# Two transformer blocks on one core: modulation parts summed in one bank, attention values and branch lifts made turned, first input product by block, first query in halves

## The chip, the core and the metric

The kernel runs on one core of a Trainium2 chip. The core has five engines that run their own instruction streams and meet at semaphores: PE (matrix products, PSUM as its output), DVE (vector work), ACT (scalar functions), POOL (here: a little arithmetic and the gathers) and SP (it issues the other DMAs). The metric is the device time of one execution in microseconds. All arithmetic is float32; the profile shows each PE product as two records.

PSUM is one tensor `ps` of 8 banks of 128 x 512 values. The main buffer in the core's memory is `big`; the program's tiles are ranges of it, so the profile writes `big` for most of them.

## What is computed

The reference, cut to its parts that the change touches:

```python
def first_block(x, ...):                      # x: 1 x 256 x 1024
    h = rmsnorm(x, norm_mix)
    aq, ak, av, hq, hf_f, hf_b, hi, hg, gate_pre = split(h @ w_in)
    ...                                       # norms and rotary positions of q, k
    y_att = gqa_attention(q, k, v) @ w_up_att     # 8 heads, 2 groups, width 64
    y_hg = hgrn2_bidirectional(...) @ w_up_hg
    gts = sigmoid(gate_pre)                   # two gates of width 1024
    merged = gts[0] * y_att + gts[1] * y_hg
    x = x + merged @ w_out
    x = x + peer_ffn(rmsnorm(x, norm_ffn), ...)
    ...
def peer_ffn(h, w_q, sub_keys, u, v):         # per token: 8 heads x 16 experts of 16384
    q = h @ w_q
    s = einsum(q, sub_keys)                   # 8 heads x 2 halves x 128 scores
    idx, g = ...                              # top 16 of sums of two top 16
    a = <u[idx], h>;  w = gelu(a) * g;  return sum of w * v[idx]
def second_block(x, c, ...):
    mod = silu(c) @ w_ada + b_ada             # 6 parts of 1024
    sh_m, sc_m, gt_m, sh_f, sc_f, gt_f = split(mod)
    h = modulate(rms_norm(x, g_mix), sh_m, sc_m)
    ...                                       # mixer, then a gated feed-forward
```

## The kernel before

The 256 tokens are two blocks of 128 rows (`NB`), the width 1024 is eight chunks of 128 (`KD`). One layer of each block is computed. Nothing is scheduled by a program: every engine's stream is written by hand, and PE's order is repeated in `product_list`. That list numbers every result that PE leaves in a bank; `product_done` counts them, `bank_list` deals them to banks in turn (eight ahead of the query, then four, since two pairs of banks hold the sums of the experts), and `begin` waits until the bank's last user has emptied it (`bank_emptied`). `wait_product` and `wait_moved` are the waits for a result and for its removal.

**Weights.** `tile_list` is the order of the weight tiles, each up to 1024 x 512 values (2.1 MB). They go through a ring of three slots (`wring`, `W_SLOTS`). SP issues them in that order (L442) and waits before each until the tile that held the slot has had its last product. `w_up_hg` (L435) and the `subkeys` (L440) have places of their own and stand in the same queue. x, the lane constants and the identity are issued ahead of the first tile `in_hf`.

**The first stage** up to the query runs on PE in this order: the normed x turned (`n1T`), products of h with the tiles of `w_in`, by columns of the weight (`by_cols`, L509: the weight is stationary and 256 tokens move, the result is turned) or by rows (`by_rows`, L497: 512 columns of the weight move, tokens on the partitions). Then attention: scores `a_S` (L558), ACT's exponentials, transposes of the probabilities (`probs_turned`, L548), values (`attended`, L570: eight heads x two blocks of keys, 64 columns each), DVE divides by the sums (`attention_in`), and PE turns the result (`attended_turned`, L579). Then the eight levels of the gated scan (`level`, L589), with the products of the branch gates `in_g0` to `in_g3` between them, `g_O` (L662), a norm on DVE and ACT, and its transposes `g_OT` (L673).

Spread among these are eight parts of `mod` that are needed as columns: `ada_part(i)` (L523) multiplies silu(c), repeated 32 times in `c_rep`, with a tile, four chunks at a time on four 32-column strips of the array, which leaves partial sums on the partitions; ACT moves them out, and `ada_col(i)` (L531) adds the four strips and turns them with four products of one column. Four more parts are needed as rows, in the second block (`ada8` to `ada11`).

`lifted(b, h)` (L686) makes the two lifts of block b, half h, by rows; DVE combines them with the gates into `merged`, PE turns it (`turn_merged`, L486), ACT moves it to `hT`, and `out0`, `out1` follow by rows.

**The query.** DVE adds `out0` and `out1` to x, ACT and DVE norm it, PE turns it (`turn_query`), and `query("peer_q0", 0)` (L716) and `score(0, 0)` (L727) make the scores of the first two heads. ACT moves both. DVE's `route_first(0)` finds the experts of head 0 of all 128 rows (from L1668 on) and writes 16 indices a row. From these POOL starts gathers (L1364), each of one pair of expert rows for 128 tokens, 1.05 MB, into a ring of ten slots. Gathers 0 to 9 wait for indices alone (the tenth also for `out1` of block 1). Gather 10 waits until PE has used the first pair. Per batch of four pairs DVE makes the dot products (L1763), ACT the diagonals (L1185), PE the products (`experts`, L747), and a bit of the next heads' search and query stands between the batches. PE's order ahead of the first `experts` is `peer_q0`, `keys`, `out1` of block 1, `peer_q1`, `keys`, `peer_q2`, `residual` (L754). The slot of `peer_q2` is the one that `out1` leaves.

## Time and profile before

| | |
|---|---|
| median of 3 runs | 1412.82 us (1412.06 to 1413.28) |
| profiled execution | 1411.05 us |
| its span, first to last instruction | 1409.0 us |
| PE busy | 1273.0 us, 90% |
| DVE, POOL, ACT busy | 52%, 23%, 17% |
| mean granted clock of PE | 0.964 |

The profiled execution is 1.8 us under the median, and 2.05 us of it lie outside the span. A granted clock of 1.00 is the 2.4 GHz level of PE, 0.50 the 1.2 GHz level. In the tables a row gives the start and the length of a group of like instructions, and in brackets how long its engine had been idle and what ended that.

### The profile page before, as it was taken

How to read it: one execution, taken by the hardware profiler on the slowest of the kernel's cores; microseconds unless marked ns; L12 is line 12 of the kernel's file. 1: busy time of each engine (PE TensorE's matmuls, PEld its weight loads, DVE VectorE, ACT ScalarE, POOL GpSimd, SP SyncE). 2: the span in 40 equal slices, each digit the busy share in tenths (PEclk: the TensorE clock that was granted, in tenths of full speed). 3: DMA queues.
4: the chain of work that ended last, by engine and by line, in shares of the span. 5: the costliest groups of instructions: out<-in, count | busy, mean ns of one | idle time of the engine just before them, and what ended most of it. 6: DMA issues, size and time to landing. Idle time of an engine off the chain costs nothing.

```text
span 1409.0 us, 12608 instructions
## 1 busy us (share of the span) xinstructions
PE 1273.0 (90%) x4558; PEld 730.9 (52%) x4558; DVE 726.7 (52%) x1752; ACT 238.8 (17%) x611; POOL 324.6 (23%) x273
## 2 busy tenths in 40 slices
PE   7999999988988878788799887878999899999998
PEld 6757554574554444333333333333465468988743
DVE  3664623178777777787786865653255242100001
ACT  2132221121111111112221112112112421000000
POOL 0100000024544544354444454540000000000000
PEclk9999999999999999899999998999999989999999
DMA  8534576369999999999999999995344723552530
GB/s 289 176 123 180 179 277 245 120 269 421 390 419 421 421 416 420 416 421 401 417 422 421 411 415 421 420 422 216 120 166 166 263 78 120 179 180 95 204 145 34
DMA packets 98380, 398.72 MB, mean 283 GB/s; under 512 B 6353, under 2 KB 9809, under 8 KB 65425
## 3 DMA queue, kind: packets, MB, share of 16 engines
q0 software_dynamic: 37376, 270.29, 46.4%
q1 hardware_dynamic: 60944, 127.65, 25.4%
q8 instruction: 37, 0.61, 0.2%
q14 instruction: 23, 0.18, 0.0%
HBM read 396.86 MB, written 1.05 MB: 282 GB/s over the span
## 4 chain that ended last, share of the span: by engine, by line
PE 60%; DMA 22%; DVE 12%; issue 2%; ACT 2%; POOL 1%; DVEq 0%; SPq 0%; ACTq 0%
DMA big<-in_peer_uv,idx_t 21%; PE ps L497 16%; PE ps L509 14%; PE ps L747 11%; DVE big L1763 6%; PE ps L998 5%; PE ps L716 2%; PE ps L686 2%; PE ps L962 2%; PE ps L523 1%; PE ps L589 1%; POOL big L1364 1%; PE ps L486 1%; DMA wring<-in_w_ada 1%; ACT rows L1185 1%
## 5 line engine op out<-in xcount | busy, mean ns | idle before, releaser
L747 PE MATMUL ps<-big,rows 128*128 128x512 f32 x1024 | 489.0, 634 | 105.4 <-ACT rows L1185 105.4
L1364 POOL DMA_INDIRECT big<-in_peer_uv,idx_t x256 | 312.0, 1219 | 388.9 <-PE ps L747 323.5
L747 PEld LDWEIGHTS ps<-big,rows 128*128 128x128 f32 x1024 | 202.7, 203 | 374.0 <-issue 374.0
L1763 DVE CUSTOM_DVE_ANT_0 big<-big 128x1024 f32<-128x1024 f32 x256 | 307.8, 1225 | 145.5 <-DMA big<-in_peer_uv,idx_t 142.5
L497 PE MATMUL ps<-wring,big 128*128 128x512 f32 (+1 forms) x560 | 240.5, 586 | 2.6 <-DMA wring<-in_w_in 1.1
L509 PE MATMUL ps<-big,wring 128*128 128x256 f32 x896 | 195.7, 381 | 1.0 <-DVE big L1418 1.0
L509 PEld LDWEIGHTS ps<-big,wring 128*128 128x128 f32 x896 | 171.2, 191 | 25.3 <-issue 1.9
L497 PEld LDWEIGHTS ps<-wring,big 128*128 128x128 f32 x560 | 105.6, 191 | 125.8 <-issue 121.0
L1179 ACT ACTIVATE small<-small 128x4 f32<-128x4 f32 x64 | 13.2, 206 | 514.7 <-DVE small L1768 514.7
L1185 ACT ACTIVATE rows<-const,small 128x128 f32<-128x128 f32 x256 | 81.8, 390 | 19.2 <-DVE small L1772 18.0
L998 PE MATMUL ps<-wring,big 128*128 128x512 f32 x176 | 75.7, 592 | 0.0
L716 PEld LDWEIGHTS ps<-big,wring 128*128 128x128 f32 x512 | 63.6, 199 | 14.6 <-issue 13.6
L716 PE MATMUL ps<-big,wring 128*128 128x128 f32 x512 | 64.8, 283 | 4.6 <-issue 3.7
L1043 ACT ACTIVATE big<-ps 128x512 f32<-128x512 f32 x73 | 40.9, 592 | 153.7 <-PE ps L486 61.7
L998 PEld LDWEIGHTS ps<-wring,big 128*128 128x128 f32 x176 | 33.4, 190 | 41.7 <-issue 41.6
L1956 DVE SCALAR_TENSOR_TENSOR big<-ps,big 128x512 f32<-128x512 f32 x8 | 5.5, 692 | 93.1 <-PE ps L998 70.6
L1987 DVE TENSOR_TENSOR big<-big,ps 128x512 f32<-128x512 f32 x11 | 7.6, 688 | 82.1 <-PE ps L509 74.8
L1375 POOL TENSOR_TENSOR big<-big,rows 128x1024 f32<-128x1024 f32 x2 | 4.7, 2342 | 149.8 <-ACT big L1043 142.9
L1343 POOL DMA_DIRECT2D rows<-in_norm_ffn x1 | 0.7, 686 | 149.1 <-DVE big L1625 149.1
L1984 DVE SCALAR_TENSOR_TENSOR big<-big,ps 128x512 f32<-128x512 f32 x11 | 7.6, 688 | 46.9 <-ACT big L1327 46.9
L1327 ACT ACTIVATE big<-ps 128x512 f32<-128x512 f32 x11 | 6.6, 597 | 136.4 <-DVE big L1987 63.3
L962 PEld LDWEIGHTS ps<-big,wring 128*128 128x128 f32 x256 | 28.8, 192 | 0.5 <-issue 0.5
(241 smaller groups left out, 921.9 us busy)
## 6 DMA issues: line engine op xcount, KB each, us to landing
wring<-in_w_in SPq DMA_DIRECT2D x17, 2048.0 KB, 8.3
wring<-in_w_ada SPq DMA_DIRECT2D x12, 2048.0 KB, 8.5
wring<-in_w_gate SPq DMA_DIRECT2D x5, 2048.0 KB, 7.7
wring<-in_w_up SPq DMA_DIRECT2D x5, 2048.0 KB, 7.7
wring<-in_w_down SPq DMA_DIRECT2D x5, 2048.0 KB, 7.6
wring<-in_w_out SPq DMA_DIRECT2D x4, 2048.0 KB, 15.1
wring<-in_peer_wq SPq DMA_DIRECT2D x4, 2048.0 KB, 8.0
big<-in_peer_uv,idx_t POOLq DMA_INDIRECT x256
```

What stands on the lines that cost most here:

```text
L486: last = nc.tensor.transpose(o[:, c * P:(c + 1) * P], src[:, b, (4 * h + c) * P:(4 * h + c + 1) * P], ident)
L497: last = nc.tensor.matmul(o[:, 0:w], lhs[:, c, b * P:(b + 1) * P], wt[:, c, c0:c0 + w], start=(c == 0), stop=(c == k - 1))
L509: last = nc.tensor.matmul(o[:, c2 * S:(c2 + 1) * S], wt[:, c, n0:n0 + P], src[:, c, :], start=(c == 0), stop=(c == KD - 1))
L686: last = nc.tensor.matmul(o, lhs[:, c, b * P:(b + 1) * P], wt[:, c, h * 512:(h + 1) * 512], start=(c == 0), stop=(c == 3))
L716: last = nc.tensor.matmul(o[:, n * P:(n + 1) * P], wt[:, c, n * P:(n + 1) * P], h2T[b][:, c, :], start=(c == 0), stop=(c == KD - 1))
L747: last = nc.tensor.matmul(banks[h], diag[:, k % DIAGS, :], v_part[:, ring_at(k), h * 512:(h + 1) * 512], start=False, stop=(k % SLOTS == S ...
L962: last = nc.tensor.matmul(o[:, c2 * S + b * P:c2 * S + (b + 1) * P], wt[:, c, n0:n0 + P], hT2[:, c, b * P:(b + 1) * P], start=(c == 0), st ...
L998: last = nc.tensor.matmul(o, gT[:, f, b * P:(b + 1) * P], wt[:, c, h * 512:(h + 1) * 512], start=(f == 0), stop=(f == FC - 1))
L1043: nc.scalar.activation(dst, bank(name, n) if src is None else src, ACT.Copy).then_inc(emptied(*name), 1)
L1185: nc.scalar.activation(diag[:, k % DIAGS, :], ident, ACT.Copy, scale=w_now[:, at_w:at_w + 1])\
L1364: pool.indirect_dma_start(pair_ring[:, ring_at(k), :], None, a["peer_uv"], bass.IndirectOffsetOnAxis(idx_t[:, k:k + 1], 0))\
L1763: nc.vector.tensor_tensor_reduce(u_part[:, ring_at(k), :], u_part[:, ring_at(k), :], h_t[:, b, :], 1.0, 0.0, ALU.mult, ALU.add, a_dot[:, i ...
```

## The change

- **Modulation parts.** `c_wide` has 40 columns a chunk, zero but for column 8. Taking 32 of them from column 8 - i on puts silu(c) on partition i of each strip. So parts 0 to 7 are added into one bank (bank 7, which nothing else uses up to the query; the others are dealt to seven banks). One move, one group of four products against `part_sums` and one more move make all eight. The slot of a part 0 to 6 is now freed by a count of its own, `ada_used`.
- **Attention values turned.** DVE multiplies the probabilities with the reciprocals ahead of their transposes (`normalised`), and `attended` makes the values turned: per block of keys and group one product of 512 columns, on the upper or lower 64 partitions of the result. ACT moves it to `yT`. `attention_in` and `attended_turned` go.
- **Lifts turned.** `in_g0` to `in_g3` and both lifts are made by columns, DVE combines them straight in `hT`, and the transposes of `merged` go. The second half of `in_g3` moves behind `g_O`, `ada6` behind `g_OT`, `ada7` among the lifts. `out0` of block 0 starts when three of four parts of `merged` are there, and `out0` of block 1 is split around the query's transposes.
- **First input product by block.** `in_hf` is made for block 0 before block 1 is turned, and x's second block is issued behind the tile `in_hf`.
- **First query in halves.** `peer_q0` and its scores for block 0 are made, moved and searched one head at a time.

The core of the diff:

```diff
@@ product_list
+    p += [("g_O", 0), ("g_O", 1), ("in_g3", 1), ("g_OT", 0), ("g_OT", 1)]
+    p += [("up_hg", 0), ("up_hg", 1), ("up_att", 0), ("ada7",), ("up_att", 1)]
+    p += [("up_hg", 2), ("up_att", 2), ("up_hg", 3), ("up_att", 3)]
...
@@ SP
-            sp.dma_start(x[:, 1, :], a["x"][P:S, :]).then_inc(x_landed[1], 16)
             sp.dma_start(ident, a["const"][:, C_IDENT:C_IDENT + P]).then_inc(ident_landed, 16)
...
-                    if before.startswith("down"):
+                    if before.startswith("ada") and int(before[3:]) < ADA_COLS - 1:
+                        sp.wait_ge(ada_used, int(before[3:]) + 1)
+                    elif before.startswith("down"):
...
+                if n == 0:
+                    sp.dma_start(x[:, 1, :], a["x"][P:S, :]).then_inc(x_landed[1], 16)
@@ PE
             def ada_part(i):
                 wt = tile(f"ada{i}", KD, 512)
-                o = begin(f"ada{i}")
+                cols_ = i < ADA_COLS
+                o = ps[:, BANK[("ada7",)], :] if i < ADA_COLS - 1 else begin(f"ada{i}")
+                lo = ADA_COLS - i if cols_ else ADA_COLS
...
-                last.then_inc(product_done, 1)
-
-            def ada_col(i):
-
-                wait_moved(pe, f"ada{i}")
-                o = begin("ada_col", i)
+                last.then_inc(ada_used if i < ADA_COLS - 1 else product_done, 1)
+
+            def ada_col():
+
+                wait_moved(pe, "ada7")
+                o = begin("ada_col")
...
                 o = begin("a_Y", b)
-                for h in range(AH):
-                    for s_b in range(NB):
-                        g = h % 2
-                        last = nc.tensor.matmul(o[:, h * HD:(h + 1) * HD], a_PT[:, s_b, h, :],
-                                                qkv[:, s_b, 640 + g * HD:640 + (g + 1) * HD],
+                for s_b in range(NB):
+                    for g in range(AKV):
+                        last = nc.tensor.matmul(o[g * HD:(g + 1) * HD, :],
+                                                qkv[:, s_b, 640 + g * HD:640 + (g + 1) * HD], a_PT[:, s_b, g:AH:AKV, :],
                                                 start=(s_b == 0), stop=(s_b == NB - 1))
                 last.then_inc(product_done, 1)
-
-            def attended_turned(b):
-                pe.wait_ge(a_out, b + 1)
...
+            by_block("in_hf", 0, hT)
+            pe.wait_ge(h_ready, 2)
+            turn("n1T", h_t, [1])
+            wait_turned("n1T", [1])
+            by_block("in_hf", 1, hT)
...
+            reserved("out0", 1)
+            merged_out(0, 1, range(0, 5))
             turn_query(0)
+            begin("out0", 1)
+            merged_out(0, 1, range(5, 8)).then_inc(product_done, 1)
             wait_turned("n2T", [0])
-            query("peer_q0", 0)
...
+            o = begin("peer_q0", 0, 0)
+            first_query(0, o)
+            first_query(1, o).then_inc(product_done, 1)
+            first_query(2, reserved("peer_q0", 0, 1))
             pe.wait_ge(keys_landed, 16)
-            score(0, 0)
+            first_score(0)
+            first_query(3, begin("peer_q0", 0, 1)).then_inc(product_done, 1)
+            first_score(1)
             by_rows("out1", hT, blocks=[1])
@@ DVE
+            def normalised(b):
                 for n in range(4):
                     wait_moved(dve, "a_S", b, n // 2, n % 2)
                 s8 = sum1[:, 8 * b:8 * b + 8]
                 link(nc.vector.reciprocal(s8, s8))
+                tt(a_P[:, b], a_P[:, b], s8.unsqueeze(2).to_broadcast([P, AH, S]), ALU.mult).then_inc(a_normed, 1)
```

How PE's order moves, in two places. First from the first half of `in_g3` and the last level to the first lifts. Before (L523 is `ada_part`, L531 `ada_col`, L497 the second half of `in_g3`, L662 `g_O`, L673 `g_OT`, L686 the lifts):

```order
L497 MATMUL ps<-wring,big 128x512 x8
L523 MATMUL ps<-wring,c_rep 32x512 x8
L531 MATMUL ps<-const,big 128x1 x4
L662 MATMUL ps<-big 128x128 x16
L523 MATMUL ps<-wring,c_rep 32x512 x8
L531 MATMUL ps<-const,big 128x1 x4
L523 MATMUL ps<-wring,c_rep 32x512 x8
L531 MATMUL ps<-const,big 128x1 x4
L673 MATMUL ps<-const,big 128x128 x8
L531 MATMUL ps<-const,big 128x1 x4
L686 MATMUL ps<-wring,big 128x512 x4
L686 MATMUL ps<-big 128x512 x4
```

And in the changed kernel (L526 `ada_part`, L667 `g_O`, L510 the second half of `in_g3`, L675 `g_OT`, L690 the lifts, those with `wring` being `up_att`):

```order
L526 MATMUL ps<-wring,c_wide 32x512 x16
L667 MATMUL ps<-big 128x128 x16
L510 MATMUL ps<-big,wring 128x256 x16
L675 MATMUL ps<-const,big 128x128 x8
L526 MATMUL ps<-wring,c_wide 32x512 x8
L690 MATMUL ps<-big 128x256 x16
L690 MATMUL ps<-big,wring 128x256 x8
L526 MATMUL ps<-wring,c_wide 32x512 x8
L690 MATMUL ps<-big,wring 128x256 x8
```

The second half of `in_g3` now stands behind `g_O`, and with it the moment at which its slot is free for `ada7`, behind which `up_att` is queued on SP.

Second, PE from `out0` of block 0 to `peer_q1`. Before (L497 rows of `out0`, `out1`, L486 transposes, L716 query, L727 scores):

```order
L497 MATMUL ps<-wring,big 128x512 x8
L486 MATMUL ps<-const,big 128x128 x8
L497 MATMUL ps<-wring,big 128x512 x16
L486 MATMUL ps<-const,big 128x128 x8
L716 MATMUL ps<-big,wring 128x128 x32
L727 MATMUL ps<-big 128x128 x4
L497 MATMUL ps<-wring,big 128x512 x8
L716 MATMUL ps<-big,wring 128x128 x32
```

And in the changed kernel (L710 products of `out0`, L536 `ada_col`, L498 `out1`, L758 and L766 the first query and its scores, L733 `peer_q1`):

```order
L710 MATMUL ps<-wring,big 128x512 x5
L487 MATMUL ps<-const,big 128x128 x8
L710 MATMUL ps<-wring,big 128x512 x3
L758 MATMUL ps<-big,wring 128x128 x24
L766 MATMUL ps<-big 128x128 x2
L758 MATMUL ps<-big,wring 128x128 x8
L766 MATMUL ps<-big 128x128 x2
L498 MATMUL ps<-wring,big 128x512 x8
L733 MATMUL ps<-big,wring 128x128 x32
```

The scores of the first head now stand ahead of the last quarter of the query; `out1` of block 1 and all behind it keep their places.

## Rows read from the trace of the kernel before

**Rows 1.** The page, DMA rate in 40 equal slices of the span.

```profile
GB/s 289 176 123 180 179 277 245 120 269 421 390 419 421 421 416 420 416 421 401 417 422 421 411 415 421 420 422 216 120 166 166 263 78 120 179 180 95 204 145 34
```

**Rows 2.** The page, chain that ended last, share of the span by engine.

```profile
PE 60%; DMA 22%; DVE 12%; issue 2%; ACT 2%; POOL 1%; DVEq 0%; SPq 0%; ACTq 0%
```

**Rows 3.** Groups by form, PE, 0 to 340 us: busy, mean ns, idle before.

```profile
L716 PE MATMUL ps<-big,wring 128*128 128x128 f32 x208 | 27.8, 295 | 4.6 <-issue 3.7 <-ACT big L1043 0.8
...
L523 PE MATMUL ps<-wring,c_rep 128*32 128x512 f32 x128 | 15.4, 598 | 0.0
...
L531 PE MATMUL ps<-const,big 128*128 128x1 f32 x64 | 8.5, 253 | 0.0
...
L570 PE MATMUL ps<-big 128*128 128x64 f32 x64 | 7.4, 275 | 0.0
...
L673 PE MATMUL ps<-const,big 128*128 128x128 f32 x8 | 1.3, 286 | 1.4 <-DVE big L1633 1.4
...
L579 PE MATMUL ps<-const,big 128*128 128x128 f32 x8 | 1.0, 272 | 0.0
```

**Rows 4.** Timeline of PE at the first lifts: start, length, group.

```profile
220.42 0.66 PE L673 MATMUL ps<-const,big 128*128 128x128 f32 x4 [1.39 <-DVE big L1633]
...
222.17 6.61 PE L686 MATMUL ps<-wring,big 128*128 128x512 f32 x8
228.61 3.60 PE L686 MATMUL ps<-big 128*128 128x512 f32 x8
```

**Rows 5.** Windows: length, busy PE, PEld, DVE, ACT, POOL, PEclk, DMA, GB/s.

```profile
222.00:223.00 1.00, 1.00 (x3) 0.65 (x4) 0.00 (x0) 0.17 (x1) 0.23 (x1) 0.50 0.92 365
```

**Rows 6.** Start of the program: timeline of PE, then one window.

```profile
13.30 29.42 PE L509 MATMUL ps<-big,wring 128*128 128x256 f32 x128 [1.02 <-DVE big L1418]
...
0.00:10.00 10.00, 1.94 (x8) 1.57 (x8) 2.95 (x7) 6.17 (x12) 0.18 (x4) 1.00 0.81 285
```

**Rows 7.** Two tiles issued together: SP's first issue, window at the end.

```profile
186.03 0.37 SPq L435 DMA_DIRECT2D big<-in_w_up_hg  x1
...
198.00:199.00 1.00, 1.00 (x12) 0.13 (x4) 0.18 (x1) 0.00 (x0) 0.00 (x0) 1.00 0.40 135
```

**Rows 8.** Timeline of PE: peer_q0, first records of peer_q2, residual.

```profile
276.82 7.38 PE L716 MATMUL ps<-big,wring 128*128 128x128 f32 x64 [0.79 <-ACT big L1043]
...
302.16 3.85 PE L716 MATMUL ps<-big,wring 128*128 128x128 f32 x33
...
316.99 1.88 PE L754 MATMUL ps<-x_t,const 128*128 128x512 f32 x4
```

**Rows 9.** Issues: POOL's gathers 0 and 10; SP's tile peer_q2.

```profile
296.85 1.04 POOL L1364 DMA_INDIRECT big<-in_peer_uv,idx_t  x1 [42.06 <-DVE idx_t L1721]
...
320.86 0.95 POOL L1364 DMA_INDIRECT big<-in_peer_uv,idx_t  x1 [11.60 <-PE ps L747]
...
L442 SPq DMA_DIRECT2D wring<-in_peer_wq x1: 368/368/368, 293.0 to 293.0; - x1
```

**Rows 10.** Timeline of DVE ahead of the first search.

```profile
268.33 0.69 DVE L1655 SCALAR_TENSOR_TENSOR x_t<-ps,x_t 128x512 f32<-128x512 f32 x1 [6.98 <-PE ps L497]
270.93 1.28 DVE L1411 SCALAR_TENSOR_TENSOR big<-x_t,rstd,rows 128x1024 f32<-128x1024 f32 x1 [1.91 <-ACT rstd L1039]
...
286.73 0.29 DVE L1668 MAX8 big<-big 128x8 f32<-128x128 f32 x1 [10.84 <-ACT big L1043]
```

**Rows 11.** DMA queues (packets, MB, share): 294 to 297, 299 to 300, 375 to 377.

```profile
q1 hardware_dynamic: 405, 0.83, 85.8%
...
q0 software_dynamic: 3, 0.02, 6.3%
...
q0 software_dynamic: 92, 0.66, 78.5%
q1 hardware_dynamic: 92, 0.19, 24.1%
```

**Rows 12.** Timeline of PE in the expert stage, after a longer idle stretch.

```profile
434.90 8.80 PE L747 MATMUL ps<-big,rows 128*128 128x512 f32 x16 [2.15 <-ACT rows L1185]
```

More of the change, by code:

```diff
@@ L58 @@
 C_GROUP = C_ONE + 1
[L59 removed]
+C_PART = C_GROUP + P
+C_END = C_PART + ADA_COLS
 L_LB = 0
@@ L651, in _ @@
                     ada_part(i + 1)
-                if n % 2 == 0 and i:
-                    ada_col(i + 1)
-            by_rows("in_g3", hT, blocks=[1])
             ada_part(5)
-            ada_col(4)
             pe.wait_ge(g_filled, 1)
@@ L664, in _ @@
                 last.then_inc(product_done, 1)
-            ada_part(6)
-            ada_col(5)
-            ada_part(7)
-            ada_col(6)
+            by_cols("in_g3", halves=[1])
             for b in range(NB):
@@ L674, in _, with lifted @@
                 last.then_inc(product_done, 1)
[L675 removed]
+            ada_part(6)
             for b in range(NB):
[L678 removed]
                 wait_moved(pe, "g_OT", b)
[L680 removed]
             pe.wait_ge(up_hg_landed, 16)
[L682 to L684 removed]
+            def lifted(name, h):
+                lhs, wt = (yT, tile("up_att", 4, D)) if name == "up_att" else (oT, up_hg)
+                o = begin(name, h)
+                for c2 in range(2):
+                    n0 = (2 * h + c2) * P
@@ L694, in _ @@
-            lifted(0, 0)
-            lifted(0, 1)
-            lifted(1, 0)
-            turn_merged(0)
-            lifted(1, 1)
-            wait_turned("mT", [0])
-            by_rows("out0", hT, blocks=[0])
-            turn_merged(1)
+                last.then_inc(product_done, 1)
+            lifted("up_hg", 0)
+            lifted("up_hg", 1)
+            for b in range(NB):
+                wait_moved(pe, "a_Y", b)
+            lifted("up_att", 0)
+            pe.wait_ge(const_landed, 32)
@@ new lines, in _, with merged_out @@
+            ada_part(7)
+            lifted("up_att", 1)
+            for h in (2, 3):
+                lifted("up_hg", h)
+                lifted("up_att", h)
+            def merged_out(i, b, chunks):
+                wt = tile(f"out{i}", KD, 512)
+                o = ps[:, BANK[(f"out{i}", b)], :]
+                for c in chunks:
+                    last = nc.tensor.matmul(o, hT[:, c, b * P:(b + 1) * P], wt[:, c, :], start=(c == 0),
+                                            stop=(c == KD - 1))
+                return last
@@ L702, in _ @@
+            reserved("out0", 0)
+            pe.wait_ge(merged_ready, 3)
+            merged_out(0, 0, range(0, 6))
+            pe.wait_ge(merged_ready, 4)
+            begin("out0", 0)
+            merged_out(0, 0, range(6, 8)).then_inc(product_done, 1)
+            ada_col()
             by_rows("out1", hT, blocks=[0])
-            wait_turned("mT", [1])
-            by_rows("out0", hT, blocks=[1])
             def turn_query(b):
@@ L1192, in _ @@
             query_turned(0)
-            query_out(0, 0)
-            scores_out(0, 0)
+            for h in range(2):
+                c = slice(2 * h, 2 * h + 2)
+                for name, dst in ((("peer_q0", 0, h), pqT), (("keys", 0, 0, h), sc[(0, 0)])):
+                    move(dst[:, c, :], *name, src=bank(name, 2 * P).rearrange("p (c t) -> p c t", c=2))
             best(0)
```

245 lines of the change are left out of this document (111 added, 134 removed).

## Prediction, made before the run

> **What bounds the kernel now.** I read the page first: its 40 slices and the chain that ended last. In the slices the rate of the DMA engines is the thing to see [rows 1]. It goes up and down until the tenth slice, stands at 390 to 422 GB/s from there to slice 27, and falls again. The chain that ended last is mostly PE [rows 2], and between 332 and 971 us it alternates between gathers, dot products and PE. So there are three stages. Up to the first gather at 296.85 us [rows 9] PE is busy nearly without a break. From there to about 966 us, 256 gathers of 1.05 MB pass at the rate of the DMA engines. After that PE is the bound again, and the change moves nothing there that I can price above zero: `c_wide` is as wide in a product as `c_rep` was, and the products of `gate0` and `up0` are the same code under another name. Work taken from PE ahead of the first gathers moves everything behind it, if the gathers are fed as before. That "if" is the second half of this prediction.
>
> I sum against the profiled execution (1411.05 us) and add 1.8 us at the end, since the median is 1412.82. Q is the start of the first query product, 276.82 us now [rows 8].
>
> **PE ahead of Q: what goes.** The rows by form give the busy time of each kind [rows 3]. A group overlaps the next by some 0.1 us, and I subtract that.
> - Attention values: 64 records of 64 columns take 7.4 us, the same 275 ns as a record of 128 columns, so narrow products are paid in full. Now it is 4 products a block of 512 columns on 64 columns of the array, and the two groups can run beside each other. No row shows column tiles of 64. Bounds: `ada_part` on tiles of 32 takes 1.9 us for 16 records (15.4 us for 128), which is four at once; with no overlap, 8 records of 0.43 us are 3.4. I take 1.9 us a block, a saving of 3.3 in all; the other end is 0.1.
> - `ada_col`: 8.5 us for eight groups, 7.6 without overlap. One group of four stays: -6.6.
> - Transposes: those of the attention values (L579, 1.0 us of records, 0.9 net) and of `merged` (twice as many, 1.8): -2.7.
> - The idle 1.4 us ahead of the second `g_OT` transposes [rows 3, 4]. They come 7.7 us after `g_O` ends, by a chain of DVE and ACT that stays. Now 6.9 us of `in_g3` and 0.45 of the first transposes stand in that gap: -1.0.
> - Behind that idle time the granted clock is 0.50, the 1.2 GHz level, and 8 records of the first lift take 6.61 us where the next 8 take 3.60 [rows 4, 5]. With the gap filled by dense products I take this away: -3.2. The other end is nothing.
> - The 0.8 us in which PE waited for ACT ahead of the query [rows 3] is covered by three products of `out0`: -0.8. DVE adds `out1` of block 0 at 268.33, 0.2 after the product, and ends the scaled row for the query at 272.2 [rows 10], 4.1 after the product; five products of `out0` take 4.3, so PE just doesn't wait for it.
>
> Together 17.6 us.
>
> **PE ahead of Q: what comes.**
> - `in_hf` by block. PE begins it now at 13.30, when both blocks are turned [rows 6]. Later it begins when block 0 is turned (about 9.7 us) and the tile has landed. By 10 us the engines have moved 2.85 MB [rows 6]. Without x's second block ahead of it the tile ends at 2.75 MB, so at 9.75 us; I add 1.3 us until the landing is seen, an assumption: 11.0. Half of the tile's products take 7.1, 1.8 more at the low clock, then 2.4 for the second block's transposes and their moves, then 7.1: the end is 29.5 instead of 28.9. +0.6, between -0.7 and +1.5.
> - `ada5` is now used 12.3 us after the last of `in_g2`, and is the second of two tiles issued then. The pair issued at 186.03 ended on the DMA engines at 198.4 [rows 7], 12.4 us later, and lands about 0.5 after: +0.4.
> - `up_att` is the larger one. Its transfer stands in SP's queue behind `ada7`, which needs `in_g3`'s slot, and `in_g3`'s last product has moved behind `g_O`. So both tiles are issued at that product's end, and `up_att` lands 12.7 us later by the same pair. PE needs it after 0.45, 0.4 idle, 0.45, `ada6` 1.85 and two lifts 6.9, that is after 10.1. +2.6. Nothing on PE can pass it. An idle stretch of 2.15 us elsewhere is followed by 16 records in 8.80 us, where two times 3.60 less the overlap make 7.0 [rows 4, 12]: +1.8.
> - Lifts, gate products by columns, DVE's two products with the reciprocals (2.4 us each, in front of transposes that have 4 us to spare) and ACT's extra table loads cost nothing: PE's own work hides them. Uncovered, the two DVE products would be 4.8.
>
> Together 5.4 us. So Q and all up to `out1` of block 1 come **12.2 us earlier**.
>
> The Trainium skill ("TensorE: Matmul & The Clock Gate", Measured speedup vs the span model) has three column tiles at 2.38 times the speed of one, 0.79 of ideal. Two tiles at 0.79 would take 2.2 us instead of 1.9, and the sum would be 0.6 us worse; `ada_part`'s own row is nearer to ideal, and I stay with it.
>
> **The query in halves.** DVE starts its search now 9.9 us after Q (286.73) [rows 10]. With halves it is 3.6 for two products' worth, 1.8 for the third, which hides ACT's move, 0.7 for half of the scores and 0.45 for their move: 6.6. The search takes 9.8 us either way, so the first gather is issued at Q+16.7 instead of Q+20.0.
>
> One might take these 3.3 us as a gain. But the DMA engines are full from 294.75 on, first with `peer_q2`, whose slot is free when `out1` of block 1 is done (issued at 293.0 [rows 9]). The first bytes of a gather appear only at 299.9 [rows 11], and `peer_q2` ends at 300.3: it had a lead of 5.1 us and passed alone. The engines' full stretch starts no earlier relative to Q, so the earlier gathers bring nothing, and they take `peer_q2`'s lead: 2.1 us are left, in which 0.77 of its 2.10 MB pass (0.83 MB by 297.0 now [rows 11]). Beside gathers a tile gets 0.19 MB in 2 us, equal packets but small ones [rows 11]. The other 1.33 MB need 13 to 14.5 us, and it lands at Q+34 to Q+35. PE wants it at Q+25.3 (302.16) [rows 8]. A **stall of about 9 us** on PE.
>
> Behind it: 7.1 for the products, some 2.2 for the low clock after such a gap, 1.7 for the residual, and the first expert products free a ring slot, 2.2 after which gather 10 is issued: Q+47.5. Now that is Q+44.0 (320.86) [rows 9], since today the same products take 14.8 us, from 302.16 to 316.99 [rows 8], with 3.7 us of idle time that nothing shown ends [rows 3]. If these 3.7 come again, it is Q+51.2. The ten gathers and the tile are 12.6 MB and end at Q+48.1; gather 10's bytes come 3.0 after its issue. So the engines stand idle 2.2 to 5.9 us, and the next batch, which has under 1 us to spare, loses some more. **+4.5 us**, which the engines don't make up.
>
> Sum: 1411.05 - 12.2 + 4.5 + 1.8 = 1405.2.
>
> The skill ("DMA: Bandwidth & Descriptors", Queues, rings and completion order) has the engines take turns between queues by the packet. By that rule the tile gets its share in packets, and the rows have 92 against 92; an equal share by bytes would leave a stall of under 2 us and give some 1401.
>
> **Rivals.**
> - No collision: the tile keeps enough of its lead, or PE's stall is hidden by DMA engines that are full anyway. For it: each microsecond of lead is worth 4.5 us of transfer. Then the 4.5 fall away: 1400.7.
> - The removals are worth less: the 64-column tiles don't overlap (3.2 us) and the clock still falls at `g_OT` (3.2), because the same short transposes stand there. 1411.6.
> - The tile loses its whole lead. This is the slower one. Decisive point: the first gather's bytes come no later than the tile's, that is 2.1 us sooner than I put them. All 2.10 MB then pass at 0.09 MB/us, landing at Q+41.8; with the low clock and the 3.7 us again, gather 10 is issued at Q+58.7, 14.7 later than now. 1411.05 - 12.2 + 14.7 + 1.8 = 1415.4. Against it: SP issues the tile at Q+15.9, and a gather's first bytes took 3.0 us [rows 9, 11].
>
> **How the numbers follow.** Forecast 0.62, no collision 0.20, smaller removals 0.12, lead lost 0.06. The range takes the forecast's ends, the block-wise `in_hf` and the collision from 2.2 to 9, and reaches past the first rival and short of the second: 1399.5 to 1411.0. A measurement of this kernel can tell about 0.2%, 2.8 us, from no change. Faster by more: 0.84, from the first two cases less the forecast's slow tail, and a little of the third. Within: 0.11. Slower: 0.05.
>
> **What the profile after would show.** `a_Y` groups of about 1.9 us; no idle time at `g_OT` over 0.5 and a clock of 1.00 there; a PE wait of about 2.6 us for a tile in the middle of the lifts; Q near 264.6; the first gather 16.7 after Q; PE idle about 9 us ahead of `peer_q2`'s products, the tile's bytes running beside gathers at a quarter of the rate; a dip of the DMA engines some 48 us after Q; the stage behind 971 us unchanged at 438 us. I am wrong on the whole if the dip is missing or much longer, or if Q isn't 10 us or more earlier.

## Result, and the profile after

| | before | after |
|---|---|---|
| median, us | 1412.87 (1412.06 to 1413.28) | 1405.45 (1404.28 to 1406.13) |
| ratio, 95% interval | 1 | 0.9945 (0.993 to 0.996) |
| profiled execution, us (span) | 1411.05 (1409.0) | 1405.89 (1403.7) |
| start of the first query product (Q) | 276.82 | 268.19 |
| gather 0 issued | 296.85 = Q+20.0 | 284.73 = Q+16.5 |
| gather 10 issued | 320.86 = Q+44.0 | 313.97 = Q+45.8 |
| last gather issued | 954.72 | 948.46 |

The change makes the kernel 7.4 us faster, which is 0.2 us from the forecast. The profile shows that this closeness is in part luck: two terms of opposite sign were both too large, by some 3 us each. By the prediction's own last sign ("if Q isn't 10 us or more earlier") it was wrong on the whole: Q is 8.6 us earlier. Medians are used below for what an edit is worth, the traces for where it goes.

The page of after has the three stages of before: DMA rate in 40 slices, then the chain that ended last.

```profile
GB/s 286 158 147 180 180 263 261 128 357 393 404 420 421 421 415 420 418 421 411 421 420 421 394 411 421 422 421 172 120 169 164 262 81 122 180 179 100 200 148 32
...
PE 57%; DMA 24%; DVE 12%; issue 2%; ACT 2%; POOL 1%; another core or an unknown queue 1%; SPq 0%; DVEq 0%
```

Against [rows 1], the engines fill earlier (357 where 269 stood in the ninth slice), and the tenth slice is lower (393 for 421). The first is the gain, the second is where a part of it goes.

PE's groups by form, 0 to 340 us: busy, mean ns, idle before. They answer to [rows 3].

```profile
L604 PE MATMUL ps<-big,wring 128*128 128x128 f32 x128 | 17.6, 307 | 3.6 <-DMA wring<-in_w_in 2.7 <-DVE big L1433 1.0
L690 PE MATMUL ps<-big,wring 128*128 128x256 f32 x64 | 16.3, 414 | 2.9 <-DMA wring<-in_w_up_att 2.9
...
L526 PE MATMUL ps<-wring,c_wide 128*32 128x512 f32 x128 | 15.4, 598 | 1.4 <-DMA wring<-in_w_ada 1.4
...
L573 PE MATMUL ps<-big 128*64 128x512 f32 x16 | 3.9, 605 | 0.0
...
L744 PE MATMUL ps<-big 128*128 128x128 f32 x16 | 3.1, 358 | 8.8 <-ACT big L1071 8.8
...
L675 PE MATMUL ps<-const,big 128*128 128x128 f32 x8 | 1.3, 279 | 0.3 <-DVE big L1644 0.3
...
L536 PE MATMUL ps<-const,big 128*128 128x8 f32 x8 | 1.0, 246 | 0.0
```

The attention values (L573) cost 3.9 us where 7.4 stood. `ada_col` (L536) costs 1.0 for 8.5. The transposes of `g_OT` (L675) wait 0.3 for 1.4. In their place come waits for tiles: 2.7 at `in_hf`, 1.4 at an ada part, 2.9 at `up_att`, and 8.8 at a score product.

PE's timeline at these places: `in_q` behind `in_hb` (of before, then of after), `ada5`, the lifts, the first query product, the scores of `peer_q1`.

```profile
42.56 20.80 PE L497 MATMUL ps<-wring,big 128*128 128x512 f32 x64
```

```profile
44.72 20.80 PE L498 MATMUL ps<-wring,big 128*128 128x512 f32 x64
...
195.39 1.92 PE L526 MATMUL ps<-wring,c_wide 128*32 128x512 f32 x16 [1.42 <-DMA wring<-in_w_ada]
...
211.19 7.17 PE L690 MATMUL ps<-big 128*128 128x256 f32 x32
221.29 5.38 PE L690 MATMUL ps<-big,wring 128*128 128x256 f32 x16 [2.93 <-DMA wring<-in_w_up_att]
...
228.45 3.72 PE L690 MATMUL ps<-big,wring 128*128 128x256 f32 x16
...
268.19 5.52 PE L758 MATMUL ps<-big,wring 128*128 128x128 f32 x48
...
299.92 2.07 PE L744 MATMUL ps<-big 128*128 128x128 f32 x8 [8.78 <-ACT big L1071]
```

The start of after is 2.2 us later than that of before at `in_q`, so the removals gave 8.6 + 2.2 = 10.8 us net of the other waits. The issues of gathers 0 and 10 on POOL, ACT's move that PE waited for, windows of the dip behind gather 10 (length, busy time of PE, PEld, DVE, ACT, POOL, granted clock, DMA share, GB/s), and the two queues at 290 to 292 us:

```profile
284.73 1.04 POOL L1379 DMA_INDIRECT big<-in_peer_uv,idx_t  x1 [27.88 <-DVE idx_t L1745]
...
313.97 1.60 POOL L1379 DMA_INDIRECT big<-in_peer_uv,idx_t  x1 [16.83 <-PE ps L789]
...
299.27 0.60 ACT L1071 ACTIVATE big<-ps 128x512 f32<-128x512 f32 x1 [11.82 <-remote]
...
314.00:317.00 3.00, 3.00 (x9) 1.33 (x8) 3.00 (x7) 0.00 (x0) 2.69 (x2) 1.00 0.95 325
317.00:320.00 3.00, 3.00 (x17) 2.04 (x16) 1.77 (x8) 0.23 (x1) 2.39 (x3) 1.00 0.92 371
...
q0 software_dynamic: 82, 0.67, 81.2%
q1 hardware_dynamic: 80, 0.16, 21.5%
```

The tile of `peer_q2` (queue q1) passes beside the gathers (q0) with as many packets and a fifth of the bytes, as forecast. The dip is there too: 325 and 371 GB/s where [rows 1] has 421. But it is small: 0.44 MB under 421 GB/s from 314 to 320 us, worth about 1.0 us. What the forecast hadn't is ACT's idle time of 11.8 us, which ends by nothing that the profile knows. It means that PE in this execution stood 8.8 us ahead of the scores, for ACT, and never for the tile itself. Is it that, or the tile, which costs the time? And is the collision worth 4.5 us?

### The profile page after: what moved, and what is told of

Its sections match the earlier page's. It is cut to its first block, busy times and chain, and to the rows that moved or that the text cites. A ratio compares the mean times of both kernels' runs of the same rounds, so it can differ in the third digit from the quotient of the medians.

```text
span 1403.7 us, 12831 instructions
## 1 busy us (share of the span) xinstructions
PE 1257.9 (90%) x4686; PEld 752.9 (54%) x4686; DVE 730.3 (52%) x1753; ACT 234.1 (17%) x597; POOL 321.2 (23%) x273
## 4 chain that ended last, share of the span: by engine, by line
PE 57%; DMA 24%; DVE 12%; issue 2%; ACT 2%; POOL 1%; another core or an unknown queue 1%; SPq 0%; DVEq 0%
DMA big<-in_peer_uv,idx_t 20%; PE ps L510 16%; PE ps L789 11%; PE ps L498 11%; DVE big L1787 6%; PE ps L1026 5%; PE ps L604 3%; DMA wring<-in_w_ada 2%; PE ps L690 2%; DMA wring<-in_w_in 1%; PE ps L733 1%; PE ps L526 1%; PE ps L710 1%; DMA wring<-in_w_up_att 1%; POOL big L1379 1%
## 5 line engine op out<-in xcount | busy, mean ns | idle before, releaser
L1379 POOL DMA_INDIRECT big<-in_peer_uv,idx_t x256 | 308.6, 1205 | 384.3 <-PE ps L789 336.2
L510 PE MATMUL ps<-big,wring 128*128 128x256 f32 x1088 | 237.0, 379 | 0.0
L510 PEld LDWEIGHTS ps<-big,wring 128*128 128x128 f32 x1088 | 205.9, 190 | 29.7 <-issue 2.2
L498 PE MATMUL ps<-wring,big 128*128 128x512 f32 (+1 forms) x400 | 169.3, 580 | 2.8 <-ACT big L1071 1.6
L498 PEld LDWEIGHTS ps<-wring,big 128*128 128x128 f32 x400 | 75.6, 191 | 88.6 <-issue 83.7
L1199 ACT ACTIVATE rows<-const,small 128x128 f32<-128x128 f32 x256 | 81.8, 390 | 19.2 <-DVE small L1796 18.0
L733 PEld LDWEIGHTS ps<-big,wring 128*128 128x128 f32 x448 | 54.5, 196 | 9.1 <-issue 9.1
L1026 PEld LDWEIGHTS ps<-wring,big 128*128 128x128 f32 x176 | 33.4, 190 | 41.7 <-issue 41.6
L1071 ACT ACTIVATE big<-ps 128x512 f32<-128x512 f32 (+1 forms) x64 | 34.9, 577 | 123.0 <-PE ps L498 30.3
L733 PE MATMUL ps<-big,wring 128*128 128x128 f32 x448 | 54.7, 279 | 0.0
L604 PE MATMUL ps<-big,wring 128*128 128x128 f32 x384 | 46.5, 286 | 3.6 <-DMA wring<-in_w_in 2.7
L604 PEld LDWEIGHTS ps<-big,wring 128*128 128x128 f32 x384 | 46.1, 202 | 4.7 <-issue 3.5
```

The source lines that it names most:

```text
L498: last = nc.tensor.matmul(o[:, 0:w], lhs[:, c, b * P:(b + 1) * P], wt[:, c, c0:c0 + w], start=(c == 0), stop=(c == k - 1))
L510: last = nc.tensor.matmul(o[:, c2 * S:(c2 + 1) * S], wt[:, c, n0:n0 + P], src[:, c, :], start=(c == 0), stop=(c == KD - 1))
L604: last = nc.tensor.matmul(o[:, c2 * S + b * P:c2 * S + (b + 1) * P], wt[:, c, n0:n0 + P], src[:, c, b * P:(b + 1) * P], start=(c == 0), st ...
L733: last = nc.tensor.matmul(o[:, n * P:(n + 1) * P], wt[:, c, n * P:(n + 1) * P], h2T[b][:, c, :], start=(c == 0), stop=(c == KD - 1))
L1026: last = nc.tensor.matmul(o, gT[:, f, b * P:(b + 1) * P], wt[:, c, h * 512:(h + 1) * 512], start=(f == 0), stop=(f == FC - 1))
L1071: nc.scalar.activation(dst, bank(name, n) if src is None else src, ACT.Copy).then_inc(emptied(*name), 1)
```

## Experiments

"The changed kernel" is after. Readings of all runs stand in one table. MB is what the DMA engines moved from 280 to 600 us, the sum of windows of 20 us. At some 0.42 MB/us it tells how far the stage of the gathers has come at 600 us. The ratios go by runs of before that were taken beside each set, with medians of 1412.01 us (e1 to e4), 1411.88 (e5 to e8) and 1411.83 (e9 to e12); so medians of different sets compare only to about 1 us.

| run | edit | median, us | ratio to before (95%) | Q | gather 10 | MB to 600 |
|---|---|---|---|---|---|---|
| before | | 1412.87 | | 276.82 | Q+44.0 | 127.8 |
| after | | 1405.45 | 0.9945 (.993-.996) | 268.19 | Q+45.8 | 130.2 |
| e8 | after once more | 1404.31 | 0.9938 (.9923-.9952) | 267.66 | Q+45.3 | 130.9 |
| e1 | query whole | 1403.51 | 0.9941 (.9928-.9955) | 267.26 | Q+42.8 | 131.6 |
| e2 | before, query halved | 1413.30 | 1.0014 (1.0002-1.0026) | 277.35 | Q+45.0 | 128.0 |
| e4 | tile ahead of gathers | 1406.46 | 0.9963 (.995-.9977) | 267.31 | Q+46.4 | 130.0 |
| e3, e10 | `in_hf` whole | 1408.98, 1408.45 | 0.9984 (.9975-.9993), 0.9975 (.9965-.9986) | 268.63, 270.69 | Q+44.7, 45.3 | 130.7, 129.7 |
| e12 | ACT's program shifted | 1402.81 | 0.9932 (.9914-.9949) | 267.10 | Q+44.4 | 131.1 |
| e5 | `up_att` ahead | 1399.61 | 0.9911 (.9898-.9925) | 263.11 | Q+46.4 | 132.3 |
| e6 | `ada5` first | 1401.66 | 0.9923 (.9909-.9936) | 264.89 | Q+45.7 | 131.7 |
| e9 | halves, both orders | 1398.26 | 0.9901 (.9885-.9918) | 262.90 | Q+43.9 | 133.3 |
| e7, e11 | whole, both orders | 1397.82, 1398.72 | 0.9895 (.988-.991), 0.9905 (.9889-.9922) | 261.68, 261.33 | Q+42.6, 43.1 | 133.9, 134.0 |

**The query whole again (e1).** `peer_q0` of block 0 goes back to one bank, one product and one score.

```diff
-            o = begin("peer_q0", 0, 0)
-            first_query(0, o)
...
-            first_score(1)
+            query("peer_q0", 0)
+            pe.wait_ge(keys_landed, 16)
+            score(0, 0)
```

> The changed kernel with its first query and scores whole again, as in the kernel before (PE, ACT and DVE); all else as changed. Q stays at 268.2 us. Collision theory: with the whole query the tile of peer_q2 is issued at about Q+16.2 and the first gather at Q+20.0, so the tile keeps its lead of 5 us, lands by about Q+24.5, PE's stall of 8.8 us ahead of keys(0,1) and peer_q2 goes to under 1 us, gather 10 is issued at about Q+44, and the time falls by the 4.5 us that the stage lost: about 1401.0 us. Rival A, the halves bring what they were meant to (the first gather 3.3 us earlier) and the stage's loss comes from elsewhere: 3.3 us slower than the changed kernel, about 1408.7. Rival B, the loss belongs to ACT's idle time of 11.8 us that has its own cause (it was 3.05 us in the kernel before): the stall comes again in this kernel and the time stays within 1 us of 1405.5.

The tile's wait is gone, as the collision has it. In PE's timeline the products of `peer_q2` follow the scores at once, but the experts' first products then wait for ACT. Gather 10 and the same windows as above:

```profile
292.13 7.31 PE L733 MATMUL ps<-big,wring 128*128 128x128 f32 x64
299.28 1.88 PE L776 MATMUL ps<-x_t,const 128*128 128x512 f32 x4
306.29 8.64 PE L769 MATMUL ps<-big,rows 128*128 128x512 f32 x16 [5.14 <-ACT rows L1179]
...
310.06 0.94 POOL L1357 DMA_INDIRECT big<-in_peer_uv,idx_t  x1 [10.44 <-PE ps L769]
...
314.00:317.00 3.00, 2.70 (x19) 1.98 (x17) 0.24 (x3) 1.14 (x3) 1.45 (x2) 1.00 1.02 423
```

No dip: 423 GB/s where after has 325. At 600 us it is 1.4 MB ahead of after, 3.3 us, and 0.9 of them are its earlier Q. That leaves 2.4 us for the halves in these two executions, and 1.3 against e8 (0.7 MB, less 0.4). The medians give less: 0.9941 against 0.9945 and 0.9938 is nothing that can be told from zero. That the halves take the tile's lead is shown, the price of 4.5 us is not.

**Before, with only the query halved (e2).** The same lines, the other way.

```diff
-            query("peer_q0", 0)
-            pe.wait_ge(keys_landed, 16)
-            score(0, 0)
+            o = begin("peer_q0", 0, 0)
+            first_query(0, o)
...
+            first_score(1)
```

> The kernel before with only the first query and its scores in halves, as in the changed kernel; nothing else of the change. Q stays at 276.8 us. Collision theory: first gather at about Q+16.7, tile of peer_q2 beside gathers, PE waits some 9 us for it, gather 10 comes 2 to 6 us later against Q than the 44.0 of before, and the time rises by about 4.5 us: 1417.3 us. Rival A (the earlier first gather is a gain): 3.3 us less, 1409.5. Rival B (the loss has nothing to do with the halves): within 1 us of 1412.8.

PE waits for the tile itself here, 6.6 us:

```profile
308.80 9.86 PE L716 MATMUL ps<-big,wring 128*128 128x128 f32 x64 [6.58 <-DMA wring<-in_peer_wq]
```

At 340 us this kernel is 0.7 MB behind before (19.2 to 19.9). At 380 us it is 0.2 ahead (35.9 to 35.7). What before has in hand it loses itself, a little later: one window of before, then the same of this kernel.

```profile
360.00:380.00 20.00, 19.37 (x67) 10.65 (x68) 15.84 (x49) 5.44 (x16) 10.42 (x8) 0.91 0.93 374
```

```profile
360.00:380.00 20.00, 17.87 (x69) 10.25 (x70) 15.85 (x53) 5.65 (x17) 9.92 (x9) 1.00 1.01 411
```

Both sums run from 280 us. The ring of ten gathers, which PE, DVE and ACT must turn over, loses something against 421 GB/s between 320 and 380 us in every kernel here: 1.0 MB in before, but only 0.2 to 0.4 in the others with the query whole (e7, e11, e1), and 0.7 to 1.2 in those with halves, e4 aside (0.2). So in this pair the collision's loss takes the place of another, and "which the engines don't make up" was wrong; in the pair of e1 and after there is little other loss that could cover it. Gather 10 comes at Q+45.0, only 1.0 us later than in before. By the ratio the time is 2.0 us over before (0.3 to 3.7), by the two medians of this set 1.3: less than half of the forecast's 4.5.

**The tile ahead of the gathers (e4).**

```diff
+                if k == 0:
+                    n_q2 = TILE_NO["peer_q2"]
+                    pool.wait_ge(tile_landed[n_q2 % W_SLOTS], 16 * (n_q2 // W_SLOTS + 1))
```

> The changed kernel with one wait more: GpSimd issues gather 0 only when the tile of peer_q2 has landed. Collision theory: the tile passes alone in about 5.3 us and lands at about Q+21.6 (289.8 us), PE's stall ahead of peer_q2 goes, the first gather is issued 5 us later and its first bytes come 3.0 us after that, in which the DMA engines stand idle; gather 10 isn't late any more. Net of the two about 1.5 us less than the changed kernel, 1404.0, and 3 us more than with the whole query. On ACT: if its idle time of 11.8 us ahead of the move of peer_q1's product comes from the load on the DMA engines by gathers and tile together, it is under 4 us here; if it has another cause, it is there again with 10 us or more, PE waits for it again, and the time is 3 to 5 us above the changed kernel's, since the gathers start later.

The window in which the DMA engines stand nearly idle, then PE's timeline:

```profile
290.00:295.00 5.00, 4.31 (x39) 4.12 (x38) 4.62 (x19) 2.58 (x4) 2.63 (x3) 1.00 0.35 97
```

```profile
291.95 7.31 PE L733 MATMUL ps<-big,wring 128*128 128x128 f32 x64
299.09 1.88 PE L796 MATMUL ps<-x_t,const 128*128 128x512 f32 x4
309.72 8.96 PE L789 MATMUL ps<-big,rows 128*128 128x512 f32 x16 [8.74 <-ACT rows L1199]
```

The wait for the tile is gone and stands one product later: the first experts have no gathered rows yet, and gather 10 comes at Q+46.4, later than in after. It is 1 to 3.5 us slower than the changed kernel (1405.45 and, in another set, 1404.31 us) and not 1.5 faster. Protecting the tile in this way costs no less than the collision does. ACT's idle time ahead of the move is 3.75 us here, not 11.8.

**ACT's 11.8 us (e8, e12).** e8 is the changed kernel itself; e12 has 32 waits more in ACT's program, on a semaphore long at its value, where ACT stands idle.

```diff
             log_and_exp()
+            for _ in range(32):
+                act.wait_ge(lane_landed, 16)
```

> The changed kernel itself once more, beside the others on one chip. Expected 1405.4 us. Every theory that has ACT's 11.8 us of idle time ahead of peer_q1's move as a property of this kernel expects it again at 287 to 299 us. The other theory: it belongs to the one execution, since the kernels with the query whole and with the tile first have nothing like it; then ACT moves peer_q1's product at about 291.2 us here, PE waits 6 to 7 us for the tile itself, and the time is the same within 1 us because the tile was late in both.

> The changed kernel with 32 more wait instructions in ACT's program, on a semaphore that is long at its value, where ACT stands idle (behind the move of ada_col): only the place of what follows in ACT's program changes. Theory A, ACT's idle time of 11.8 us ahead of the move of peer_q1's product is the loading of its next instructions beside the gathers: it is gone from there or stands at another instruction, ACT moves the product at about 291.5 us, and PE waits 6 to 7 us for peer_q2's tile itself. Theory B, it belongs to this move (a semaphore or a port): 11.8 us again at the same instruction. Either way the tile holds PE until about 299 to 300 us, and the time is within 1 us of the changed kernel's 1404.3.

ACT's timeline of e8, of e12 and of e9 at this move, then PE's in e12:

```profile
298.69 0.60 ACT L1071 ACTIVATE big<-ps 128x512 f32<-128x512 f32 x1 [11.77 <-remote]
```

```profile
290.09 0.60 ACT L1071 ACTIVATE big<-ps 128x512 f32<-128x512 f32 x1 [3.74 <-PE ps L733]
```

```profile
285.89 0.60 ACT L1074 ACTIVATE big<-ps 128x512 f32<-128x512 f32 x1 [3.74 <-PE ps L736]
```

```profile
298.23 9.54 PE L733 MATMUL ps<-big,wring 128*128 128x128 f32 x64 [6.33 <-DMA wring<-in_peer_wq]
```

The idle time isn't of one execution alone: 11.82 in after, 11.77 in e8, 11.82 in e5, 11.76 in e6. With 32 waits in front of the place it is gone. But that doesn't show that the place in ACT's program decides. The edits of e3, e10, e4 and e9 touch PE, SP or POOL alone and leave ACT's program as it is in the changed kernel, and there too ACT moves the product 3.7 us after its last work, as soon as PE has made it. e9 differs from e5, which has the idle time, only in the place of one issue on SP some 90 us earlier, and the DMA engines are as full; a packet of the queue q14, of kind instruction, passes between 288 and 289 us in both. So neither theory is shown and neither is excluded: the cause of the 11.8 us stays open. In e12 PE waits 6.3 us for the tile. `peer_q2` starts at 298.23 in e12 and at 301.20 in e8, and Q differs by 0.6. So the idle time had up to 2.4 us of its own in the trace, and gather 10 comes 1.0 us nearer to Q. At 600 us e12 is 0.2 MB ahead, which its earlier Q explains; the medians, 1402.81 and 1404.31, are nearer than the intervals can part. What the idle time costs in the end can't be told from zero.

**`in_hf` whole (e3, e10).** x's second block is issued ahead of the first tile, both blocks are turned, and the products go over both.

```diff
-            by_block("in_hf", 0, hT)
...
-            turn("n1T", h_t, [1])
-            wait_turned("n1T", [1])
-            by_block("in_hf", 1, hT)
+            by_cols("in_hf")
```

> The changed kernel with in_hf as before: x's second block issued ahead of the first weight tile, both blocks turned, then the products by columns over both blocks. Theory from the trace (in_hb began at 30.9 us in the changed kernel and at 28.7 before): in_hb begins 2.2 us earlier, everything behind it up to the first query too, and the time is 2.2 us less than the changed kernel's, about 1403.2. By the forecast's own term (0.6) it would be 1404.9; the rival is that the 2.2 us are taken up by a wait later (for a tile of the input products or for DVE), so the time stays at 1405.5.

> The changed kernel with in_hf whole, once more, for a second profile: the first profile was of the fastest of its executions (span 1403.9, the others up to 1410.4). Theory: in_hf by block and in_hf whole give the same Q, since the waits for ada5 and up_att take up what PE is early (in the first profile 1.9 and 4.2 us against 1.4 and 2.9): Q at 268 to 269 again, and a median at the level of the changed kernel, 1404 to 1406. Rival: the median of 1409.0 is a property of this kernel; then the profile shows where 4 us go, in a longer wait for a tile ahead of Q or in a longer stage of the gathers.

The 2.2 us didn't come, and the kernel is some 4 us slower than the changed one (0.9984 and 0.9975 of before, against 0.9945 and 0.9938), though the changed kernel didn't run in either of these two sets. It begins `in_q` at 43.4 and 42.7 us, up to 2.0 earlier than after. PE's timeline of e3 and of e10 at `ada5` and `up_att`:

```profile
194.58 1.92 PE L525 MATMUL ps<-wring,c_wide 128*32 128x512 f32 x16 [1.90 <-DMA wring<-in_w_ada]
...
221.72 5.38 PE L686 MATMUL ps<-big,wring 128*128 128x256 f32 x16 [4.19 <-DMA wring<-in_w_up_att]
```

```profile
194.15 3.58 PE L525 MATMUL ps<-wring,c_wide 128*32 128x512 f32 x16 [2.18 <-DMA wring<-in_w_ada]
...
222.76 6.41 PE L686 MATMUL ps<-big,wring 128*128 128x256 f32 x16 [3.98 <-DMA wring<-in_w_up_att]
```

Being early buys a longer wait for `ada5`. In e10 that wait is 2.2 us, and behind it the granted clock is 0.50, the 1.2 GHz level; in e3 it is 1.9 us and the clock stays. The same microsecond, of e10 and of e3:

```profile
195.00:196.00 1.00, 1.00 (x12) 0.34 (x8) 0.00 (x0) 0.00 (x0) 0.00 (x0) 0.50 1.05 408
```

```profile
195.00:196.00 1.00, 1.00 (x16) 0.26 (x8) 0.00 (x0) 0.00 (x0) 0.00 (x0) 1.00 0.97 356
```

The part takes 3.58 us for 1.92, the last product of `in_g3` and with it the issue of `up_att` come later, and Q is as late as 270.7. The executions of this kernel spread more than those of after (spans 1403.7 to 1410.4 us). The profiled one of e3 was the shortest of its eleven, that of e10 the longest of its ten; that others lost their clock in the same way fits, but wasn't seen. There is a second piece. PE starts on `up_att` 14.1 and 13.9 us after its issue in e3 and e10, and 12.9 to 13.0 after it in after, e1, e4, e8 and e12. In the first two, and in none of the other five, a packet of another queue passes in that stretch, at 212 to 214 us of e3:

```profile
q8 instruction: 1, 0.02, 3.3%
```

3.3% of 16 engines in 2 us is 1.06 us of one engine, the size of the delay. That is two executions of one kernel against five of others, not an experiment.

**SP's order (e5, e6), and all together (e7, e11, e9).** In e5 `up_att`, whose slot `ada5` leaves at 197 us, is issued ahead of `ada7`, which has to wait for `in_g3`. The loop then goes over `issued`:

```diff
+            issued = list(enumerate(TILES))
+            i = TILE_NO["ada7"]
+            issued[i:i + 2] = issued[i + 1], issued[i]
```

In e6 `up_hg` is issued behind `ada5`:

```diff
-                if name == "ada5":
+                if name == "ada6":
```

> The changed kernel with two transfers issued in the other order on SP: up_att's, whose slot ada5 leaves at about 197 us, now ahead of ada7's, which waits until the last product of in_g3 is done at 208 us. Slots and products are the same. Theory (the up_att stall is 2.9 us and the low clock behind it 1.9 us): no wait at the lifts, all lift groups of 3.6 us, Q at 263.4 instead of 268.2, and 4.8 us less than the changed kernel. Rival: the DMA stage or a later tile takes the gain back, Q moves but the last gather and the end don't, and the time is within 1 us of the changed kernel's. Second rival: only the wait goes and the clock falls anyway, 2.9 us.

> The changed kernel with up_hg's transfer issued behind ada5's instead of ahead of it. Theory (ada5 waits 1.4 us since it is the second of two tiles issued together): the wait ahead of ada5 is under 0.2 us. If nothing else moves, 1.4 us less than the changed kernel. Rival, from the run in which in_hf was whole: PE's earlier times are taken up again at the wait for up_att, whose landing is set by the transfers and not by PE; then that wait grows by about the same 1.4 us, Q stays at 268.2 and the time within 0.5 us of the changed kernel's.

The lifts in e5, then `ada6` and the lifts in e6:

```profile
217.97 3.62 PE L693 MATMUL ps<-big,wring 128*128 128x256 f32 x16
```

```profile
208.92 1.92 PE L526 MATMUL ps<-wring,c_wide 128*32 128x512 f32 x16 [1.15 <-DMA wring<-in_w_ada]
...
219.67 3.69 PE L690 MATMUL ps<-big,wring 128*128 128x256 f32 x16 [1.73 <-DMA wring<-in_w_up_att]
```

e5 does what was expected: at the lifts no wait and no low clock, Q at 263.11 (4.6 less than e8), and a median 4.7 under e8, for 4.8 expected. The step "`up_att` 2.6 and its low clock 1.8" is confirmed as a sum and passes through to the end. e6 gives 2.65 us, more than the 1.4 of the wait. `ada5` waits no more (-1.5), `ada6` now waits (+1.2). `up_att`'s landing is tied to the end of `in_g3`, which moved along, so its wait shrank by 1.4 instead of growing, and at 1.73 us the clock held (3.69 for 5.38). My rival had the landing fixed in time and was wrong.

> The changed kernel with three edits together: first query whole, up_att's transfer ahead of ada7's, ada5's ahead of up_hg's. If the pieces add: Q at 267.3 - 4.8 - 1.4 = 261.1 us, no PE wait for a tile between 185 and 300 us, first gather at Q+20.0 = 281.1, and a time of 1403.5 - 6.2 = 1397.3 us, 15 us under the kernel before. Rival: the stage of the gathers isn't moved by its start alone, since its waits at 640 to 680 and 780 to 820 us take back part of it: then above 1400.

> The changed kernel with its halves kept and both edits of SP's order (up_att's transfer ahead of ada7's, ada5's ahead of up_hg's). Against the kernel with the same edits and the query whole (1397.8 us), it prices the halves at the earlier start. By the forecast's collision (+4.5 us): 1402.3. By the pair of runs so far (changed kernel 1404.3, with the query whole 1403.5): 0 to 1 us more, about 1398.5. Rival, the halves gain: 1396. In the trace: Q at about 262 us, no wait for up_att, gather 10 at Q+45 to 46 against Q+42.6 with the whole query.

> The kernel with the query whole and both edits of SP's order, beside its twin with halves on one chip: 1397.8 us again. If the halves cost nothing, the two are within 1 us of each other; if they cost the forecast's 4.5 us, this one is 4 to 5 us under the other.

e7's 1397.82 us was forecast at 1397.3; it is 1.0% under before, and 6 us and more under the changed kernel. The forecast took 4.8 and 1.4 for the two edits of the order. The gains that were measured, 4.7 and 2.65, don't add, since part of the wait for `up_att` and its low clock is in both: e9 is 1.4 us under e5. e9 and e11 ran on one chip: 1398.26 with halves, 1398.72 with the query whole. The halves cost nothing that these medians can tell, though PE waits for the tile as forecast. In e9 it stands ahead of `peer_q2`, in e11 ahead of the first experts.

```profile
293.99 9.11 PE L736 MATMUL ps<-big,wring 128*128 128x128 f32 x64 [6.29 <-DMA wring<-in_peer_wq]
```

```profile
300.38 9.59 PE L772 MATMUL ps<-big,rows 128*128 128x512 f32 x16 [5.15 <-ACT rows L1182]
```

With halves PE waits for the tile, with the whole query for the rows that ACT spreads, and gather 10 comes at Q+43.9 (45 to 46 was expected, but ACT's idle time isn't there) and Q+43.1. At 600 us e11 is 0.7 MB ahead, 1.7 us, and its Q is 1.6 us earlier. Either of the two is the best version here.

## Why the prediction was right, and where it wasn't

The time and its range held; the sign on Q, 10 us or more, didn't. By steps:

- **Attention values, 3.3 us: right.** The eight records of a block, four products on 64 columns of the array, begin and end in 1.94 us, and what follows begins 1.87 after the first; 1.9 was taken. The Trainium skill's 0.79 of ideal for three column tiles ("TensorE: Matmul & The Clock Gate", Measured speedup vs the span model) would make it 2.2 by estimate. Against the 3.4 us of no overlap, 1.87 is 0.92 of ideal for two tiles, and the measurement decides.
- **`ada_col`, transposes, 9.3 us: right.** One group of 1.0 us is left of 8.5; L579 and the turned `merged` are gone.
- **`g_OT`, 1.0 + 3.2 us: right.** The wait is 0.3 where [rows 4] has 1.39, the granted clock from 208 to 209 us is 1.00, and the 32 lift products behind it, 7.2 us, run at full clock. Before, the first 8 of twice the columns took 6.6. With the first point this ends the second rival.
- **`in_hf` by block, +0.6: mis-sized.** Its end was put at 29.5 and came at 30.9; against before the start loses 2.2 us, above the upper end of 1.5. The products began at 11.66, 0.7 after the 11.0 of the sum, and the first half took 10.2 us where 7.1 and 1.8 were put. In e8, the same kernel, the start loses 1.4, so it varies by 0.8 from one execution to the next. And e3 and e10 show that it can't be read as a cost of 2.2: with `in_hf` whole, Q isn't earlier.
- **`ada5`, +0.4: mis-sized**, 1.4.
- **`up_att`, 2.6 + 1.8: right**, 2.9 + 1.8 (5.38 us for the 3.62 of e5), and confirmed by e5.
- **Q, 12.2 us earlier: it was 8.6**, 9.2 in e8, and 9.5 to 9.7 in e1, e4 and e12, which are the same up to Q. So the miss is 2.5 to 3.6 us. 1.6 of the missing 3.6 is `in_hf`, 1.0 `ada5`, 0.3 `up_att`; the rest are pieces below 0.4, such as gate products by columns at 6.91 for 6.87.
- **The query in halves, +4.5: mechanism right, size wrong.** The issue times are as forecast (gather 0 at Q+16.5 for 16.7, the tile at Q+15.8 for 15.9). So is the turn by packets, 80 against 82, on which the Trainium skill's rule ("DMA: Bandwidth & Descriptors", Queues, rings and completion order) was cited; the trace agrees. PE's wait for the tile is 6.3 to 7.7 us for 9 (e12, e9, e2, e3, e10); in the changed kernel the 8.8 are a wait for ACT, which no term of the prediction had. The tile was alone for 3.6 us where 2.1 were put, which fits that it landed sooner. Gather 10 came at Q+45.8 for 47.5: `peer_q2` starts 0.7 us sooner, and the low clock behind the gap costs 1.2 for 2.2. The idle pieces of 3.7 us [rows 3], which would have made it 51.2, didn't come again. They did in e7, 4.2 us, and gather 10 was still at Q+42.6. From the prediction's own terms the idle time of the DMA engines is 2.4 to 6.1 us, not 2.2 to 5.9; the dip measured about 1.0. The step that failed is the last, that the loss isn't made up: pairs with and without halves give -1.0 us (e2 by bytes at 600 us, less the difference in Q), 0.1 (e9 and e11), 1.3 (e8 and e1), 2.4 (after and e1), and in device time +2.0 by the ratio (e2), -0.5 (e9 and e11) and about zero (e1). So it is 0 to 2 us. The first rival, no cost of the collision, is nearer in size; but the tile did lose part of its lead and PE did wait. What holds of it is that the loss is covered where another is there anyway, which only the pair of e2 and before shows.
- **The sum.** Forecast -12.2 + 4.5 = -7.7; measured about -9 at Q and 1 to 2 lost on the way. The range held because it took in both ends. The slower rival didn't occur: the tile kept those 3.6 us alone.

## What to carry to other kernels

Price a stall where the work behind it is refilled, not where it stands: a wait that goes at one place (the tile) often stands at the next (the experts' rows), and only a twin that differs in that edit tells what it was worth. A short wait for a tile is worth more than its length if the clock falls behind it, so look first at the order in which one queue issues tiles: one tile held up by another's slot cost 4.7 us, more than the new attention values gave (3.3). Work that is early by a microsecond or two in front of a fixed landing isn't a gain and may be a loss.

## What the runs showed of the hardware

- The granted clock fell behind 1.39 us of idle time at `g_OT` before [rows 4], and behind 2.18 us at `ada5` in e10. It held behind 1.90 us at the same place in e3 and 1.73 us at the lifts in e6. The length of the gap alone doesn't decide it.
- An engine can stand 11.8 us with its operands ready while the DMA engines are full (after, e8, e5, e6), and do so no more with 32 instructions more in its program (e12), or with that program unchanged (e9, e3, e10). What decides it is open. The queues of after show packets of kind instruction, 38 of 0.62 MB together on q8 and 22 on q14, which pass among the data.
- One such packet of q8 takes about 1.1 us of one DMA engine. The tiles that it met, in e3 and e10, were used about 1 us later; that the packet is the cause isn't shown.
- A gather's first bytes came about 4 us after the first issue in after (the tile ran alone until 288.9), 3.0 in before.
